# Issuing x from ScalarE's queue, and later places for the last head's work in the gate tiles

## The reference

```
hn = rms_norm(x, g_pre)
q, k, v, g_r, a, b, g_c = split(hn @ w_in)          # 2048 -> 7168 columns
o = retention(rope(q), rope(k), v, S)               # 8 heads x 128, also the new state S
ret_out = group_norm(o) * g_ret * silu(g_r)
c = causal depthwise conv(a * sigmoid(b))           # 31 taps over 1024 channels
c = silu(layer_norm(c)) @ w_pw2 + b_pw2
m = concat(ret_out, c * silu(g_c)) @ w_out
h = x + rms_norm(m, g_post)
x = h + sigmoid(h @ w_gate) * rms_norm(p[i] @ w_ple, g_ple)
```

## Time and profile before

| | |
|---|---|
| median of 3 runs | 1182.34 us |
| the profiled execution | 1182.32 us |
| its span, first to last instruction | 1180.5 us |
| PE busy | 1171.4 us, 99% |
| DVE busy | 923.2 us, 78% |
| ACT busy | 610.7 us, 52% |
| POOL busy | 81.2 us, 7% |
| DMA | 225.84 MB, mean 191 GB/s |

### The profile page before, as it was taken

One profiled execution on the slowest core, in us unless ns is written; L12 is line 12 of the kernel. 1 busy time (PEld: TensorE's weight loads), 2 busy tenths in 40 slices (PEclk: granted clock), 3 DMA queues, 4 the chain that ended last, 5 costly groups with the idle time before them and its releaser, 6 DMA issues.

```text
span 1180.5 us, 25710 instructions
## 1 busy us (share of the span) xinstructions
PE 1171.4 (99%) x10026; PEld 1160.2 (98%) x10026; DVE 923.2 (78%) x1487; ACT 610.7 (52%) x923; POOL 81.2 (7%) x102
## 2 busy tenths in 40 slices
PE   8999999999999999999999999999999999999998
PEld 8999999999999999999999999999999999999998
DVE  6999999999986543688879988999999774446863
ACT  7344655555556445544543435555665564455341
POOL 0000000000000012101120000000000000121000
PEclk9999999999999999999999999999999999999999
DMA  9666755555555654535556676555565556543462
GB/s 311 197 211 216 229 199 185 211 180 198 188 198 177 231 193 143 179 108 179 178 201 226 218 188 213 184 195 185 211 215 181 168 192 233 178 160 126 162 218 87
DMA packets 44331, 225.84 MB, mean 191 GB/s; under 512 B 6496, under 2 KB 13152, under 8 KB 20704
## 3 DMA queue, kind: packets, MB, share of 16 engines
q1 hardware_dynamic: 34832, 202.90, 50.7%
q10 hardware_dynamic: 9424, 21.90, 5.4%
HBM read 210.97 MB, written 13.81 MB: 190 GB/s over the span
## 4 chain that ended last, share of the span: by engine, by line
PE 98%; DMA 1%; DVE 1%; ACT 1%; SPq 0%; issue 0%
PE accum_all L494 30%; PE accum_all L495 29%; PE accum_all L496 29%; PE accum_all L586 1%; PE accum_all L587 1%; PE accum_all L588 1%; PE ps L561 1%; DMA x<-x_t 1%; PE ps L535 1%; PE ps L569 0%; DVE c_buf L1509 0%; PE ps L544 0%; PE accum_all L641 0%; PE accum_all L642 0%; PE accum_all L643 0%; PE ps L553 0%
## 5 line engine op out<-in xcount | busy, mean ns | idle before, releaser
L494 PE MATMUL accum_all<-a_hi,whi 128*128 128x264 f32 x2016 | 576.5, 286 | 0.0
L495 PE MATMUL accum_all<-a_lo,whi 128*128 128x264 f32 x2016 | 571.3, 283 | 0.0
L496 PE MATMUL accum_all<-a_hi,wlo 128*128 128x264 f32 x2016 | 570.9, 283 | 0.0
L1121 DVE TENSOR_TENSOR wlo<-raw,whi 128x2048 fp32r<-128x2048 f32 x182 | 420.9, 2314 | 172.0 <-ACT whi L758 171.8
L758 ACT ACTIVATE whi<-raw 128x2048 fp32r<-128x2048 f32 x182 | 347.8, 1913 | 156.9 <-DMA raw<-w_in 78.5
L494 PEld LDWEIGHTS accum_all<-a_hi,whi 128*128 128x128 f32 x2016 | 379.7, 188 | 4.0 <-issue 3.2
L495 PEld LDWEIGHTS accum_all<-a_lo,whi 128*128 128x128 f32 x2016 | 380.0, 188 | 0.8
L496 PEld LDWEIGHTS accum_all<-a_hi,wlo 128*128 128x128 f32 x2016 | 378.1, 188 | 0.0
L494 PE MATMUL accum_all<-b_hi,whi 128*128 128x264 f32 x672 | 191.0, 284 | 0.0
L495 PE MATMUL accum_all<-b_lo,whi 128*128 128x264 f32 x672 | 190.4, 283 | 0.0
L496 PE MATMUL accum_all<-b_hi,wlo 128*128 128x264 f32 x672 | 190.2, 283 | 0.0
(11 more groups left out here) (219 smaller groups left out, 1247.1 us busy)
## 6 DMA issues: line engine op xcount, KB each, us to landing
raw<-w_in SPq DMA_DIRECT2D x108, 1024.0 KB, 4.9
raw<-w_out SPq DMA_DIRECT2D x32, 1024.0 KB, 4.9
raw<-w_gate SPq DMA_DIRECT2D x32, 1024.0 KB, 4.9
s_new<-s_ret ACTq DMA_DIRECT2D x16, 512.0 KB, 3.6
ss_out<-s_new ACTq DMA_DIRECT2D x16, 512.0 KB, 2.7
raw<-w_pw SPq DMA_DIRECT2D x8, 1024.0 KB, 5.5
x<-x_t SPq DMA_DIRECT2D x4, 528.0 KB, 7.5
raw<-w_in SPq DMA_DIRECT2D x8, 256.0 KB, 8.5
```

The source lines that it names most:

```text
L494: pe.matmul(accum[bank][:, 0:R], w_hi[:, w:w + P], hi, start=k == 0, stop=False)
L495: pe.matmul(accum[bank][:, 0:R], w_hi[:, w:w + P], lo, start=False, stop=False)
L496: mm = pe.matmul(accum[bank][:, 0:R], w_lo[:, w:w + P], hi, start=False, stop=k == k_tiles - 1)
L1121: v.tensor_tensor(wlo[:, slot, :], raw[:, side, :], whi[:, slot, :].bitcast(F32), ALU.subtract).then_inc(s.lo_ready, 1)
```

## The change

The four quarters of x leave SyncE's program and are issued by ScalarE, right behind the gains; SyncE issues only the eight slab quarters. Three entries of the table `among` get other k steps; nothing else in the programs changes.

```
-        def load_x(g):
-            sp.dma_start(x[:, 4 * g:4 * g + 4, :], x_t[:, 4 * g:4 * g + 4, :]).then_inc(s.x_in[g], 16)
...
                 for g in range(4):
-                    load_x(g)
                     for j in range(2):
...
-            among = {1: {15: mean_over_channels}, 2: {5: last_values},
-                     3: {2: lambda: ret_samples(l, 7), 8: variance_sum},
+            among = {1: {15: mean_over_channels}, 2: {10: last_values},
+                     3: {6: lambda: ret_samples(l, 7), 10: variance_sum},
                      4: {9: lambda: stat_bcast(l, ST_LN), 14: lambda: ret_turn(l, 7)}}
...
         act.dma_start(vecs[:, 0, V_PRE:V_PRE + KT], vecs_d[:, 0, V_PRE:V_PRE + KT]).then_inc(s.gains_in, 16)
+        for g in range(4):
+            act.dma_start(x[:, 4 * g:4 * g + 4, :], x_t[:, 4 * g:4 * g + 4, :]).then_inc(s.x_in[g], 16)
```

## The result

The changed kernel takes 1187.19 us (median of 7 runs, 1185.85 to 1188.04); beside it the kernel before took 1182.34 (7 runs, 1181.97 to 1184.18). The ratio, with its 95% interval, is 1.0033 [1.0023, 1.0043] (the two medians alone give 1.0041): slower by 4.85 us in the medians, outside the forecast range and beyond the 0.2% that the prediction took as its bound. The profiled execution took 1187.19 us with a span of 1185.3, 4.8 more than before. In the changed file TensorE's, VectorE's and ScalarE's lines stand two to four lower in number: the first product is L621, tile 2 L637, the values' last line L549, `ret_turn` L565, `ret_state(8)` L1240.

The account below looks back on a forecast made before the run. With PE busy 1171.4 of 1180.5 us, only TensorE's idle time and restarts could be won. Start +0.3 and gate tiles +0.85 made +1.15 on 1182.32: about 1183.5 us, range 1181.4 to 1185.1.

Parts of the forecast that it names:

- What X0 now stands behind: At the start, queues take turns, so X0 lands between 5.3 and 7.1 us; 6.7 taken, against 4.85 before.
- The start: Up to tile 2's first matmul: later beginning traded for fewer gaps, +0.3 us, between -0.9 and +0.9.
- The estimate that the prediction drew from the Trainium skill: At the start, X0 waits for about one quarter: landing 5.9, first matmul 9.0, start -0.3 us.
- Rival C: TensorE's clock falls during 3.4 us idle before its first matmul: start +1.3 us, 1184.8 in all; chance 0.18.
- From X0's landing to the first matmul: At the start, 3.1 us as before, so TensorE begins at 9.8, 1.7 us later.
- The gaps behind it: Between first matmul and tile 2, gaps and restarts shrink from 1.7 us to 0.0 to 0.5.
- Tile 2's slab: Issued by SyncE some 1.2 us later, but hidden, with about a microsecond left.
- ScalarE's issues: Four more issues ahead of its table load: ready at some 4.5 us instead of 2.7, at no cost.
- The start waits for bytes, not for issues: In the fourth microsecond the DMA share is already 1.00 at 368 GB/s.
- The gate tiles: Values 5 steps later make VectorE late, delaying `ret_turn` 0.40 to 0.45 us per layer: +0.85 us in all.
- a new wait at `ret_turn`: In each layer's gate tiles, TensorE waits 0.7 us or so there instead of at the values.
- samples and variance: In the gate tiles, samples 4 steps later (1.4 us) and variance 2 steps (0.7 us) are free.

Follow-up runs that it names:

- slabs_first: Kernel before, all twelve quarters still on SyncE's queue, but each x quarter behind its two slab quarters instead of ahead: 1185.78 us, ratio 1.0022.
- x0_ahead: Kernel before with all x quarters on ScalarE's queue, X0 ahead of the gains; gate tiles as before: 1186.52 us, ratio 1.0031.
- hold_slabs: Kernel before with x quarters on ScalarE's queue behind the gains, SyncE waiting for X0 to land before issuing slab quarters: 1186.78 us, ratio 1.0034.
- gate_only: Kernel before with only the change's new gate-tile places; x issued by SyncE as before: 1183.52 us, ratio 1.0005.
- x_only: Kernel before with only the x quarters moved to ScalarE's queue; gate tiles as before: 1185.5 us, ratio 1.0024.
- after_warm: Changed kernel with 29 warm-up matmuls instead of 11, lasting until the first product: 1184.74 us, ratio 1.0023 against the kernel before.
- x0_on_sync: Kernel before, SyncE issuing X0 first, then the slab quarters, ScalarE the gains and X1 to X3; gate tiles as before: 1183.49 us, ratio 1.0004.
- gate_turn: Kernel before with the change's gate-tile places and the last head's turn moved to step 2 of tile 5; x as before: 1181.37 us, ratio 0.999.

## Why the prediction was wrong

*The step that failed* is "What X0 now stands behind", and with it the weight and price given to the clock. The start cost 3.94 us where +0.3 was forecast: 1.6 of the difference is X0's landing (the first product at 11.37, not 9.8), 2.4 is the clock, which the sum had at nothing, less 0.4 of gaps that were expected to stay.

*X0.* The step lined up the quarters as pairs, counted A0, B0 and X0 as what must be through, and took B0's old landing, 7.1, as the upper bound. X0 landed at 8.15. The bound nearly holds where one queue brings the three, 7.27 in slabs_first. It holds with two queues as well where X0 is at the head of its own, 6.55 in x0_ahead. What the step put at nothing is X0's place behind the gains: against x0_ahead X0 came 1.6 us later, of which 0.44 is the later issue and some 1.2 the place behind 8 KB. It takes the slabs beside it too, since in hold_slabs, behind the same gains but without slabs, X0 landed 3.9 us after its issue, as before. Why 8 KB ahead weigh so much when slabs run beside them no run shows; by X0's landing 1.73 MB had moved, against 1.12 in x0_ahead. The estimate that the prediction drew from the Trainium skill ("DMA: Bandwidth & Descriptors", "Queues, rings and completion order"), by which X0 would wait for about one quarter and land at 5.9, errs further on the same side.

*The clock.* Rival C happened. It had 0.18, because the clock stayed up through 1.77 us of idle and fell 3.0 us behind the last matmul at the end, and the expected 3.4 looked like a doubtful case. But 3.96 brought it down in slabs_first, and in gate_only 2.03 did, so the 1.77 was no sign of safety: the clock had risen only late in the warm-up, and 1.77 us of idle and 2.03 give no line between staying up and falling. With X0 where the forecast had it, the start would likely have lost the clock too; no run has an idle time of 3.4. Its price was put at 1.5 us of lost work, by supposing that it returns as fast as it fell. That is what x_only's execution lost; in the changed kernel's it was 2.3 to 2.4, because the matmuls ran at 0.22 from 11.37 to past 16. Forecast +0.3 for the start; had only this one term been right, +0.3 + 2.4 = +2.7, which with the gate tiles is 1185.9, beyond the range. With X0 late alone the time would have stayed inside, as after_warm's did (1184.74, with the clock kept up); it is the clock that took it out of the range.

*What held.* From X0's landing to the first matmul 3.12 us (3.1 forecast). The gaps behind it: none left (0.0 to 0.5). Tile 2's slab: issued 1.08 later (1.2), and TensorE doesn't wait for it. ScalarE's issues: its table load ends at 4.78 (3.0 + 1.28 = 4.3 by the prediction's terms), with X0 not yet there, so at no cost. "The start waits for bytes, not for issues" fits what every order of the quarters showed: x0_on_sync, x0_ahead, hold_slabs and slabs_first each moved the wait to another transfer, and none beat the order before.

*The gate tiles* went as forecast to a few hundredths: VectorE's line at 335.43 on the old scale (335.41), a new wait at `ret_turn` of 0.84 per layer (0.7), +0.86 us (+0.85); samples and variance at their later places cost nothing, as gate_turn shows, where no wait is left. The wait at the values was 0.5 us and was paid back as 1.7 at `ret_turn`; with `ret_turn` four steps later too, gate_turn keeps a gain of 1.2 us. The rows say, though no run has it alone, that with `ret_turn` in its old place no place of the values could have won anything: it began 0.06 us behind `og`, and `og` doesn't come earlier.

*Still open:* why the first microseconds carry fewer bytes when the slab quarters go first (0.63 MB by 5 us in one queue, 0.56 in two, 0.89 before). That piece sizes do it was not isolated. Nor is it settled why the clock stays down some 3 us in x_only's execution and nearly 7 in the changed kernel's after about the same idle time (4.28 and 4.72); by the windows it fell 0.3 us ahead of the first product in the one, 1.7 ahead of it in the other.

## What to carry to other kernels

Where the DMA engines are full, as here, a second queue added no bytes; it only decided who was late. So keep what is needed first alone at the head, with every small transfer that the same work needs, and count all that both queues have under way, not just what was issued ahead. TensorE's idle time before a dense stretch has a second price, the clock it restarts with: work out what the first stretch costs at the lower level, and stretch the warm-up to the first product when its input may come late. When work is moved later to remove a wait, look up who consumes it and how far that one is from the next wait: here 0.9 us of slack met a delay of 1.28, and `ret_turn`, at the end of the chain, had 0.06.

## What was not expected of the hardware

A transfer of 8 KB took 1.9 us with only x beside it (hold_slabs), 3.7 to 4.3 with large ones beside it from the start, and 7.1 behind X0 in its queue: its size said nothing. And ahead of X0, with slabs beside, the same 8 KB went with a landing some 1.2 us later (8.15 against 6.55, less 0.44 of issue). A transfer's landing came with much more data through than was ahead of it in line, 1.73 MB where X0 and what was issued ahead of it are 1.06. A clock at half for three microseconds cost nothing where the work behind it was waiting for data anyway (gate_only: tile 2 at 21.27), and 1.5 to 2.4 us where the data was there (x_only, the changed kernel). And the warm-up's own matmuls ran at the slower pace until late in it (421 ns, then 275 in after_warm).
